# Moving transfers in a one-core attention and FFN layer: ring pairs, the first FFN rows, norm weights and the chosen heads' tables

## The reference

```python
h = rmsnorm(x, g_mix_pre)
z = h @ w_in                      # 1024 -> all queries, keys, values and gates
o_a = nsa_mixer(...)              # 6 heads: compressed + chosen blocks + window of 512
o_b = dilated_mixer(...)          # 4 heads, three dilations (1, 4, 16) each
o_c = banded_attention(..., sinks=sinks)     # 6 heads, window of 128, with sinks
mix = concat([o_a, o_b, o_c]) @ w_out
x = x + rmsnorm(mix, g_mix_post)
u = causal_conv3(rmsnorm(x, g_ffn_pre) @ w_up) + conv_b      # width 2 * 2816
a, b = split(u)
x = x + rmsnorm((gelu(a) * b) @ w_down, g_ffn_post)
```

## Time and profile before

| | us |
|---|---|
| median of 3 runs (lowest to highest) | 3543.31 (3540.68 to 3545.15) |
| the profiled execution, own time | 3542.78 |
| its span in the trace | 3541.0 |
| PE matmuls busy | 3398.4 (96%) |
| DVE / ACT / POOL busy | 1386.2 / 1160.1 / 561.8 |
| mean granted clock of PE | 0.986 |
| moved by DMA | 676.15 MB, mean 191 GB/s |

### The profile page before, as it was taken

The page is one execution under the profiler, slowest core; times in us unless marked ns, Lnnn a source line. Parts: engine busy times, 40 slices in busy tenths (PEclk is TensorE's granted clock), DMA queues, the critical chain, the costliest instruction groups (busy, mean ns, idle before and its releaser), DMA issues. The chain is left out here.

```text
span 3541.0 us, 45314 instructions
## 1 busy us (share of the span) xinstructions
PE 3398.4 (96%) x16530; PEld 2709.6 (77%) x16530; DVE 1386.2 (39%) x3825; ACT 1160.1 (33%) x1979; POOL 561.8 (16%) x489
## 2 busy tenths in 40 slices
PE   8999999997998999999988999999999999999997
PEld 6888888876777866666657878887888788888886
DVE  5111101105766766666644444403440244115421
ACT  5111111115666755554532333302330133113310
POOL 1556654430000013222010000000000000000000
PEclk9999999998999999999989999999999999999999
DMA  5788975567888732332228665566556655665553
GB/s 189 262 304 319 322 246 192 199 202 182 197 196 210 157 81 73 77 80 54 75 67 274 188 221 192 193 241 231 192 193 241 230 191 194 240 230 200 193 191 119
DMA packets 298532, 676.15 MB, mean 191 GB/s; under 512 B 99184, under 2 KB 154992, under 8 KB 283888
## 3 DMA queue, kind: packets, MB, share of 16 engines
q1 hardware_dynamic: 265616, 517.93, 46.3%
q0 software_dynamic: 32704, 155.40, 12.2%
HBM read 496.06 MB, written 185.57 MB: 192 GB/s over the span
## 5 line engine op out<-in xcount | busy, mean ns | idle before, releaser
L1281 PE MATMUL a_ot_ps<-a_turned_w,vs 128*65 128x256 f32 (+3 forms) x1452 | 450.1, 421 | 1.2 <-issue 1.2
L526 PE MATMUL z_banks<-h_hi,z_w_hi 128*128 128x512 f32 x972 | 387.2, 398 | 0.0
L526 PE MATMUL z_banks<-h_lo,z_w_hi 128*128 128x512 f32 x972 | 384.4, 396 | 0.0
L526 PE MATMUL z_banks<-h_hi,z_w_lo 128*128 128x512 f32 x972 | 384.3, 395 | 0.0
L1559 PE MATMUL banks<-low,f_own 128*128 128x512 f32 x1344 | 319.4, 397 | 12.5 <-DMA f_own<-f_lo 6.6
L1559 PEld LDWEIGHTS banks<-low,f_own 128*128 128x128 f32 x1344 | 254.4, 190 | 73.3 <-issue 14.1
L1354 ACT ACTIVATE w_small<-w_small,a_negm 128x128 f32<-128x128 f32 (+3 forms) x510 | 247.0, 518 | 168.9 <-DVE a_negm L1433 104.7
L1281 PEld LDWEIGHTS a_ot_ps<-a_turned_w,vs 128*65 128x65 f32 x1452 | 179.8, 139 | 83.1 <-issue 70.5
L1433 DVE CUSTOM_DVE_ANT_0 w_small<-a_s_ps,near 128x128 f32<-128x128 f32 (+2 forms) x456 | 169.2, 393 | 175.9 <-PE a_s_ps L1245 148.7
L526 PEld LDWEIGHTS z_banks<-h_lo,z_w_hi 128*128 128x128 f32 x972 | 182.6, 188 | 44.2
L526 PEld LDWEIGHTS z_banks<-h_hi,z_w_lo 128*128 128x128 f32 x972 | 182.7, 188 | 42.7
(11 more groups left out here) (239 smaller groups left out, 6410.6 us busy)
## 6 DMA issues: line engine op xcount, KB each, us to landing
f_own<-f_hi SPq DMA_DIRECT2D x88, 512.0 KB, 3.7
f_own<-f_lo SPq DMA_DIRECT2D x88, 512.0 KB, 4.6
z_xs<-in_w_ffn POOLq DMA_DIRECT2D x33, 1024.0 KB, 8.2
f_hi<-z_v_hi POOLq DMA_DIRECT2D x33, 1024.0 KB, 4.9
f_lo<-z_xs POOLq DMA_DIRECT2D x33, 1024.0 KB, 5.6
low<-z_hi SPq DMA_DIRECT2D x48, 512.0 KB, 7.7
k_hi<-f_hi SPq DMA_DIRECT2D x44, 512.0 KB, 3.6
k_hi<-f_lo SPq DMA_DIRECT2D x44, 512.0 KB, 4.5
```

The costliest lines, as they stand in the source:

```text
L526: last = pe.matmul(banks[:, 4 * k + n, :], w[:, k, c, :], h[:, c, tok], start=(c == 0 and q == 0), stop=(c == DC - 1 and q == 2))
L1281: last = pe.matmul(ot_ps[0:out_width(g), at:at + count * P], values, rows, start=(x == 0), stop=(x == len(blocks) - 1), skip_group_check=True)
```

## The change

- `attend`, SP: the pick table is issued at the start of unit 3 in the loop, the own-block rows and `far` at the start of unit 18 (the first "c").
- `mix_out`, SP: the four ring pairs and the convolution's tables leave the place after `first_steps`. A new `step_ahead` issues pairs 0 and 1 behind step 14 and pairs 2 and 3 and the tables behind step 15. The wait for the split of the output weights goes along.
- `mix_out`, POOL: the rows of the first quarter come in eight times two transfers of 256 KB, one 512-column chunk of each part behind each of eight tiles (`hl_done` 5 to 12). PE waits for 16 transfers in place of 2, and the counts of the later quarters follow.
- `ffn`, POOL: waits until two half steps of the block are done (`pe_done` at 12) before it loads `gp` and x1. DVE waits for `gp` in the first tile of `finish` and no more at the start.

```diff
--- before.py
+++ after.py
@@ -1083,13 +1083,15 @@
             load_v(0, 1)
             load_k(1, 2)
             load_v(1, 2)
-            sp.dma_start(w_big[HD:HD + NS, 0, :], own_block[0:NS]).then_inc(own_in, 16)
-            sp.dma_start(pick, pick_bias).then_inc(pick_in, 16)
-            sp.dma_start(far[:], bias_s[0]).then_inc(far_in, 16)
             def load_w(c):
                 sp.dma_start(w_rows[c], wo_copy[c * P:(c + 1) * P, :]).then_inc(w_in, 16)
 
             for u in range(NU):
+                if u == 3:
+                    sp.dma_start(pick, pick_bias).then_inc(pick_in, 16)
+                if u == kind.index("c"):
+                    sp.dma_start(w_big[HD:HD + NS, 0, :], own_block[0:NS]).then_inc(own_in, 16)
+                    sp.dma_start(far[:], bias_s[0]).then_inc(far_in, 16)
                 if u == first_chosen:
                     load_qm(u + 1)
                 if u == NU - 1:
@@ -1665,16 +1667,20 @@
                     sp.dma_start(dst[:, s // 4, :, bass.ds((s % 4) * P, P)], src[:, ks].bitcast(F32))\
                         .then_inc(h_out[ks], 16)
 
-            first_steps(step)
-            sp.wait_ge(whi_done, DC)
-            for e in range(2):
-                sp.wait_ge(wlo_done[e], DC // 2)
-            for i in range(AHEAD):
-                load_ring(sp, ring, ring_in, f_hi, f_lo, i, i)
-            sp.dma_start(conv[:, :, 0:3], conv_w).then_inc(c_in, 16)
-            sp.dma_start(conv[:, :, 3], conv_b).then_inc(c_in, 16)
-            other_steps(sp, step)
-            step(NT, 0, NT // 2, False, NT)
+            def step_ahead(t, k, half, first, last):
+                step(t, k, half, first, last)
+                if last == NT - 2:
+                    sp.wait_ge(whi_done, DC)
+                    for e in range(2):
+                        sp.wait_ge(wlo_done[e], DC // 2)
+                if last and last < NT:
+                    for i in range(2 * (last - NT + 2), 2 * (last - NT + 2) + 2):
+                        load_ring(sp, ring, ring_in, f_hi, f_lo, i, i)
+                if last == NT - 1:
+                    sp.dma_start(conv[:, :, 0:3], conv_w).then_inc(c_in, 16)
+                    sp.dma_start(conv[:, :, 3], conv_b).then_inc(c_in, 16)
+
+            steps(sp, step_ahead)
             for k in range(2):
                 sp.wait_ge(x1_out[k], 16 * (NT // 2 + 1))
                 sp.wait_ge(h_out[k], 32 * (NT // 2 + 1))
@@ -1692,8 +1698,10 @@
             split_lower(pool, 0, 0, DC)
             for k in range(2):
                 pool.wait_ge(h_out[k], 32 * 3)
-            for dst, src in zip(f_h, (h2_hi, h2_lo)):
-                pool.dma_start(dst.bitcast(F32), src[0].rearrange("p (c n) -> p c n", n=512)).then_inc(h_in, 16)
+            for c in range(DC):
+                pool.wait_ge(hl_done, 5 + c)
+                for dst, src in zip(f_h, (h2_hi, h2_lo)):
+                    pool.dma_start(dst[:, c, :].bitcast(F32), src[0, :, c * 512:(c + 1) * 512]).then_inc(h_in, 16)
 
         @blk.scalar
         def _(act):
@@ -1829,7 +1837,7 @@
             first_steps(step)
             other_steps(pe, step)
             pe.sem_inc(pe_done, RING)
-            pe.wait_ge(h_in, 32)
+            pe.wait_ge(h_in, 32 * DC)
             pe.wait_ge(ring_in[0], 32)
             pe.wait_ge(ol_done, NT)
             up_half(pe, banks[:, 0, :], ring[0], f_h, pe_done)
@@ -1931,6 +1939,7 @@
 
             pool.memset(halo[:], 0.0).then_inc(set_done, 1)
             pool.memset(half, -0.5).then_inc(set_done, 1)
+            pool.wait_ge(pe_done, RING + AHEAD + 2)
             pool.dma_start(gp[:], g_post.partition_broadcast(P)).then_inc(g_in, 16)
             for t in range(2):
                 load_x(t)
@@ -1994,7 +2003,7 @@
 
             with pe.Fori(0, NQ - 1) as q:
                 rest(q)
-                pe.wait_ge(h_in, q * 32 + 64)
+                pe.wait_ge(h_in, q * 32 + 32 * DC + 32)
                 for j in range(2):
                     up(q + 1, j)
             rest(NQ - 1)
@@ -2043,7 +2052,6 @@
             dve.sem_inc(f_taken, TQ)
             dve.wait_ge(c_in, 32)
             dve.wait_ge(set_done, 2)
-            dve.wait_ge(g_in, 16)
 
             def up(q, j):
                 k, n = j % 2, q * NF + j
@@ -2068,6 +2076,8 @@
                 dve.tensor_tensor(g_lo[:, j, :], gt[:], g_hi[:, j, :].bitcast(F32), ALU.subtract).then_inc(glo_done, 1)
 
             def finish(q, t):
+                if t == 0:
+                    dve.wait_ge(g_in, 16)
                 dve.wait_ge(rstd_done, q * TQ + t + 1)
                 if t:
                     dve.wait_ge(out_done, q * TQ + t)
```

## The result

| | before | after |
|---|---|---|
| median (lowest to highest), us | 3541.99 (3540.46 to 3545.15), 4 runs | 3519.61 (3516.22 to 3521.43), 4 runs |
| ratio, 95% interval | 1 | 0.9935 [0.9917, 0.9952] |
| profiled execution, own time / span | 3542.78 / 3541.0 | 3516.22 / 3514.4 |

A forecast was written before the change was run, and what follows sets the result against it. PE is busy nearly everywhere; four of its idle gaps end on transfers the change touches. 8.2 + 10.7 + 5.5 + 0.4 = 24.8 us off 3542.8 gives 3518.0, as median 3518.5; range 3513 to 3526.

The forecast's parts named there:

- Part 1: Attention: moving own-block rows, pick and far tables removes the gap before the third unit and its slow clock, 8.2 us.
- 0.9 us to spare: Third attention unit: query rows would land at 866.7, before PE ends its last piece at 867.65.
- rival C: Attention: query rows still late or a sink unit waits; 3 to 4 us lost, 3522 us, chance 0.10.
- Cost taken: 0: First sink unit: moved far table and own rows delay its query load 4.9 us, still covered by 2.3 us.
- Part 2: Mixing stage: moving ring pairs and convolution tables cuts a tile from 23.7 us to 13.0, 10.7 us.
- The ring's margins: End of mixing: ring pairs 0 and 2 would land 1.4 and 1.2 us before PE wants them.
- rival A: End of mixing: ring pairs 0 and 2 late, each holding PE 1 to 2 us; 3521.5 us, chance 0.12.
- Part 3: Mixing stage: first FFN rows in eight steps cut a tile from 18.5 us to the steady period, 5.5 us.
- The delay by the steps: Mixing stage: each 0.5 MB step delays output rows 1.6 us (3.2 us per MB), inside 2.0 us spare.
- Rival B: FFN row steps: small transfers occupy engines for their whole landing time, costing 19 us; 3537.5 us, chance 0.03.
- D: FFN row steps: each of eight pays the whole load's 5.5 us, 44 in all; slower, 3562.5 us, chance 0.03.
- Part 4: Start of last stage: later norm weights and x rows shorten the first ring load from 4.97 to 4.6 us, 0.4 us.

The follow-up runs named there:

- part 1 alone: Kernel before with only the pick, own-block and far table loads moved later: 3540.8 us, 0.9988 of before.
- part 2 alone: Kernel before with only the ring pairs and the convolution's tables moved later: 3531.7 us, 0.9961 of before.
- part 4 alone: Kernel before with only the norm weights and x rows of the last stage loaded later: 3543.9 us, 0.9999 of before.

## Why the prediction was right

- **Part 1, 8.2 us.** The mechanism of the gap held: second and third unit together 39.15 us before, 30.60 after, 8.5 less, 2.65 of it in the third. The size was a little too high: with the first unit, which varies from 13.0 to 14.8 us, the three are 7.6 us shorter. The 0.9 us to spare was none in some executions (a gap of 0.84 us is left with part 1 alone), which is a little of rival C. The step that failed is "Cost taken: 0" for where the transfers go. It looked only at the loads that the moved tables stand in front of. There the cover held: the query load took 14.8 us for 9.5, 5.3 more for 4.9 in the working, and landed 1.4 us before its unit (2.3 forecast). What it missed is that without the gap the next loads meet a fuller queue. In the 10 us in which the fifth unit's table is issued the DMA share is 0.81 before (890 to 900) and 1.03 after (880 to 890), and VectorE then waits 1.35 us for the table. That cost 0.95 us in the profiled execution, up to 3 where the clock fell too. By the mean of the traces part 1 is worth 6 us, not 8.2.
- **Part 2, 10.7 us.** 23.69 to 12.95, 10.74. The ring's margins were given as 1.4 and 1.2 us. Pair 0 had 0.8; pair 2 had none and held PE for 0.3 us. The working took 0.5 us for the issue of a pair's first half and a landing of 6.3 us; pair 2 took 1.3 and 6.7. So rival A was near and came true in part, at 0.3 us and not the 3 of its price. The ring 12 us later cost 13.6.
- **Part 3, 5.5 us.** 18.48 to 12.95, 5.53. The delay by the steps was taken as 1.6 us for 0.5 MB and measured 0.7 to 1.2; for 1 MB 3.2 was expected and 3.0 seen, so the delay is not proportional to the bytes as the working had it. It also compared a store of rows with a load of outputs: such a store takes 5.4 us undisturbed (the one issued at 1909.96), so the large loads cost 6.0 us and not 6.4. Rival B, small transfers that occupy the engines for their whole landing time, falls: no step of the changed kernel holds PE, and eight transfers a step hold it by 0.3 us at most. D falls with it.
- **Part 4, 0.4 us.** The load takes 4.53 us for 4.97; the gap is 6.1 to 6.2 us in the nine profiled executions with this part and 6.5 to 7.0 in the five without. That VectorE's earlier start brings PE nothing, as said, fits: the FFN stage is 1457.6 us for 1458.1.

The chain that ended last, after, at the start of the last stage:

```profile
2052.02 4.53 DMA f_own<-f_lo
```

- **Sum.** 24.8 us forecast, 22.4 between medians, 20.3 when measured again, 26.6 between the two profiled executions. Of these 26.6, 2.1 lie ahead of the attention, where nothing was changed. The mixing line of the table has 16.1 of parts 2, 3 and 4 for 16.6 in the forecast, and 0.3 of the difference is pair 2's. With 6 us for part 1 and 0.3 off for pair 2 the same sum gives 22.3. So the mechanisms were right and one term, part 1's, was some 2 us too high. That the first median came within 1.1 us of the forecast, and the second only within 4.0, has some luck in it.

## What to carry to other kernels

Ask of each gap which transfers lie ahead of the late one in its queue, and what goes when they do. Price it by whole periods, gap and slow clock together, against a steady one: that foretold the two long tiles to within 0.1 us, and the gap in the attention to within one. When the gap goes, go through the next units of work for what is now issued closer together, small tables behind large loads first. A small transfer that is needed soon belongs ahead of the large ones, even if these must then wait a little longer for their issue.

## What the hardware showed that was not expected

- A gap of 5.6 us cost another 2.65 in work at the 1.2 GHz level, one of 8.8 us 2.0, one of 3.8 us 1.8, one of 11.3 us 2.3. In these four the cost does not grow steadily with the gap: per microsecond of it the two shorter ones cost 0.47, the two longer ones 0.2.
- Whether the clock falls can differ between executions at the same place. Before the turn of tile 8 it fell after a gap of 3.23 us with part 1 alone and not after one of 3.22 us with part 2 alone. At the first jump of the FFN's loop PE stands for 2.44 us in the kernel before and for 3.00 with part 4 alone, a place that part 4 does not touch:

```profile
2451.07 2.47 PE L1559 MATMUL banks<-low,f_own 128*128 128x512 f32 x5 [3.00 <-issue]
```

The busy time by window after it (granted clock, DMA share and GB/s last), first with part 4 alone, then before:

```profile
2453.00:2457.00 4.00, 4.00 (x11) 3.17 (x10) 2.82 (x6) 1.58 (x4) 0.00 (x0) 0.51 0.74 262
```

```profile
2452.00:2456.00 4.00, 4.00 (x19) 3.26 (x18) 2.54 (x5) 1.58 (x4) 0.00 (x0) 1.00 0.76 265
```

Eleven matmuls in 4 us against nineteen. The length of the gap alone does not decide it: at such jumps the clock stayed at 1.00 after one of 2.90 us in the changed kernel, and fell after one of 2.41 with part 2 alone. Behind its first microseconds the FFN stage keeps the full clock until its end in eight profiled executions, and takes 1456.8 to 1458.1 us; in the six where the clock falls in between it takes 1460.2 to 1466.6. This can make much of the spread of 3538 to 3546 us within one kernel; since only one execution of each was profiled, it is not shown. It is why the parts were read from periods rather than from times.
- Cutting transfers of 256 KB into 64 KB cost about 0.15 us for each transfer added. The Trainium skill, "DMA: Bandwidth & Descriptors", section "Anatomy of one DMA", has a fixed 2.0 us for each and puts most of it down to completion. These runs agree in that it is not a time for which the transfer holds up the others.
